# Scaling and transposing a normed input in one TensorE product with a diagonal matrix

## What is computed

```python
def rms_norm(x, gain, eps=1e-6):
    y = x * lax.rsqrt(jnp.mean(x * x, axis=-1, keepdims=True) + eps)
    return y * gain
# layer 0 (even) and layer 1 (odd), x: (1, 256, 1024)
h = rms_norm(x, mix_norm[l])          # one factor per row (frame), one gain per column
y = h @ w_in[l]                       # (1024, 2816) in layer 0, (1024, 3600) in layer 1
# the mixers, h @ w_out, the residual add and the MoE follow
```

## Time and profile before

| what | value |
|---|---|
| three runs | 620.03, 622.05, 623.84 us; median 622.05 |
| the profiled execution | 622.66 us, of which the span of the profile is 620.9 |
| mean granted TensorE clock | 0.958 of full |
| instructions | 11990 |
| DMA | 145.24 MB, mean 234 GB/s |

### The profile page before, as it was taken

One profiled execution on the slowest core, in us unless ns is written; L12 is line 12 of the kernel. 1 busy time (PEld: TensorE's weight loads), 2 busy tenths in 40 slices (PEclk: granted clock), 3 DMA queues, 4 the chain that ended last, 5 costly groups with the idle time before them and its releaser, 6 DMA issues.

```text
span 620.9 us, 11990 instructions
## 1 busy us (share of the span) xinstructions
PE 545.1 (88%) x5109; PEld 451.7 (73%) x5109; DVE 336.7 (54%) x593; ACT 245.2 (39%) x457; POOL 81.2 (13%) x99
## 2 busy tenths in 40 slices
PE   2899986779979888884999999999999989788986
PEld 2899985679756466641999999899989856366642
DVE  2456759974562333447599655546646562433355
ACT  3453555254433133314545642443324533133221
POOL 6600242410100000001200290001110100000000
PEclk9999997969898999999899979999998898999999
DMA  8995400013989999999565252000021999999992
GB/s 310 276 344 167 170 2 1 1 68 125 398 341 413 410 406 409 409 410 374 170 204 186 66 194 69 2 3 4 2 69 66 407 335 392 409 409 409 409 409 112
DMA packets 55893, 145.24 MB, mean 234 GB/s; under 512 B 4260, under 2 KB 29040, under 8 KB 55712
## 3 DMA queue, kind: packets, MB, share of 16 engines
q1 hardware_dynamic: 54752, 142.47, 60.7%
q0 software_dynamic: 1088, 2.00, 1.5%
HBM read 143.40 MB, written 1.05 MB: 233 GB/s over the span
## 4 chain that ended last, share of the span: by engine, by line
PE 76%; DVE 13%; ACT 5%; issue 4%; DMA 2%; POOL 1%; SPq 0%; DVEq 0%; ACTq 0%
PE PS L1830 11%; PE PS L510 7%; PE PS L1791 7%; PE PS L511 7%; PE PS L512 6%; PE PS L1852 6%; PE PS L1866 3%; PE PS L546 3%; PE PS L547 3%; PE PS L548 3%; DVE WL L506 2%; PE PS L1867 2%; DVE X L1100 2%; PE PS L2126 2%; DMA RAW<-ev_w_in 2%
## 5 line engine op out<-in xcount | busy, mean ns | idle before, releaser
L506 DVE TENSOR_TENSOR WL<-RAW,WH 128x768 fp32r<-128x768 f32 (+2 forms) x96 | 82.8, 906 | 59.0 <-ACT WH L500 57.8
L510 PE MATMUL PS<-WH,HTH 128*128 128x384 f32 (+2 forms) x272 | 91.8, 338 | 3.1 <-DVE HTL L1100 1.4
L511 PE MATMUL PS<-WL,HTH 128*128 128x384 f32 (+2 forms) x272 | 90.3, 332 | 0.0
L512 PE MATMUL PS<-WH,HTL 128*128 128x384 f32 (+2 forms) x272 | 90.1, 331 | 0.0
L1100 DVE TENSOR_TENSOR X<-PS,X 128x512 f32<-128x512 f32 (+2 forms) x84 | 52.4, 662 | 62.6 <-PE PS L1867 49.0
L500 ACT ACTIVATE WH<-RAW 128x768 fp32r<-128x768 f32 (+2 forms) x96 | 70.7, 796 | 18.2 <-PE PS L512 10.4
L510 PEld LDWEIGHTS PS<-WH,HTH 128*128 128x128 f32 x272 | 53.1, 195 | 4.7 <-DVE HTL L1100 2.2
L511 PEld LDWEIGHTS PS<-WL,HTH 128*128 128x128 f32 x272 | 53.1, 195 | 0.0
L512 PEld LDWEIGHTS PS<-WH,HTL 128*128 128x128 f32 x272 | 52.8, 194 | 0.0
L546 PE MATMUL PS<-HTH,WH 128*128 128x256 f32 x160 | 46.6, 291 | 3.8 <-DVE HTL L1100 3.8
L547 PE MATMUL PS<-HTL,WH 128*128 128x256 f32 x160 | 46.1, 288 | 0.0
(11 more groups left out here) (344 smaller groups left out, 1051.1 us busy)
## 6 DMA issues: line engine op xcount, KB each, us to landing
RAW<-moe_w_gate SPq DMA_DIRECT2D x32, 512.0 KB, 11.3
RAW<-moe_w_up SPq DMA_DIRECT2D x32, 512.0 KB, 12.3
RAW<-moe_w_down SPq DMA_DIRECT2D x32, 512.0 KB, 13.9
XG<-moe_w_gate SPq DMA_DIRECT2D x32, 512.0 KB, 14.3
XG<-moe_w_up SPq DMA_DIRECT2D x32, 512.0 KB, 14.7
XD<-moe_w_down SPq DMA_DIRECT2D x32, 512.0 KB, 14.7
RAW<-od_w_in SPq DMA_DIRECT2D x9, 1536.0 KB, 8.2
RAW<-ev_w_in SPq DMA_DIRECT2D x6, 1536.0 KB, 12.9
```

Source lines behind the costliest of these rows:

```text
L506: done(nc.vector.tensor_tensor(out=lo, in0=raw, in1=hi.bitcast(F32), op=ALU.subtract), "unit_lo")
L510: nc.tensor.matmul(ps, ah, bh, start=start, stop=False)
L511: nc.tensor.matmul(ps, ah, bl, start=False, stop=False)
L512: return nc.tensor.matmul(ps, al, bh, start=False, stop=stop)
```

## The change

X comes in two transfers, one for each tile. The identity and the gains (now GR, 16 rows of 128 for both layers, 8 KB) are fetched by ScalarE's queue. The first two of the eight k blocks of chunk 0 have a transfer of their own. TensorE transposes GR once, and ScalarE copies the result to GC, one column of gains per block k.

H is no longer computed. VectorE writes DGR, the identity times the row factors (128x128 for each tile), and TensorE computes X^T * diag(factor) as a plain float32 product of X (stationary) with DGR (moving), one PSUM bank of 128x256 per block k. ScalarE rounds it with the gain as its scale (`norm_hi`), VectorE takes the remainder in one instruction with the same gain (`norm_lo`). Both alternate with the weight units, and TensorE puts the products of unit j+2's input behind the matmuls of unit j. Before the first products TensorE runs 14 (layer 0) or 10 (layer 1) products of the identity with itself, whose result is not used (`warm`). In layer 1 the squares are taken in halves, each when its half of X is added, and VectorE norms before it takes the first weight unit instead of behind three. The broadcast of layer 1's gains is gone, and on GpSimd the two steps of `norm(0)` now come ahead of the masks' DMA.

The diff, with its indentation reduced by eight; left out are `MSQ`, `GC` and `GR`'s declarations, merged or renumbered semaphores (`mask`, `lb_d`, `pt`, `hT_ps`, `hT_hi` of the later projections), and the wait for `c_pad`, which moves from ahead of layer 1's projection into its evacuation:

```diff
@@ -155,7 +155,8 @@
...
 gb = top[0]
-GB = sb("GB", [P, D])
+top[0] += D * 4
+DGR = at("DGR", [P, NT, P], gb)
@@ -314,6 +316,7 @@
...
 PROJ_BANKS = 6
+NORM_BANK = (0, 1, 2, 3, 6, 7, 1, 2)
@@ -389,9 +392,8 @@
...
     xv = x.rearrange("b (i p) d -> p (b i) d", p=P)
-    sp.dma_start(X[:, :, :], xv).then_inc(sem("x_in"), 16)
-    sp.dma_start(CT[:, 0:P], consts[:, 0:P]).then_inc(sem("ct_in"), 16)
-    sp.dma_start(GB[:, :], mix_norm[0].partition_broadcast(P)).then_inc(sem("g0_in"), 16)
+    for i in range(NT):
+        sp.dma_start(X[:, i, :], xv[:, i, :]).then_inc(sem(f"x_in{i}"), 16)
@@ -423,8 +425,12 @@
...
                 sp.wait_ge(sem("unit_lo"), slot_units[i - SLOTS])
-            sp.dma_start(RAW[:, s, 0:KT * n].rearrange("p (k n) -> p k n", k=KT),
-                         w[0, :, c0:c0 + n].rearrange("(k p) n -> p k n", p=P)).then_inc(sem(f"landed{s}"), 16)
+            raw = RAW[:, s, 0:KT * n].rearrange("p (k n) -> p k n", k=KT)
+            src = w[0, :, c0:c0 + n].rearrange("(k p) n -> p k n", p=P)
+            if i == 0:
+                sp.dma_start(raw[:, 0:2], src[:, 0:2]).then_inc(sem("first"), 16)
+                raw, src = raw[:, 2:], src[:, 2:]
+            sp.dma_start(raw, src).then_inc(sem(f"landed{s}"), 16)
@@ -490,7 +496,9 @@
...
     u = unit_no[i, j]
-    if u == min(unit_no[i, jj] for jj in range(4)):
+    if u == 0:
+        act.wait_ge(sem("first"), 16)
+    elif u == 1 or i and u == min(unit_no[i, jj] for jj in range(4)):
@@ -602,29 +611,28 @@
...
     link(nc.gpsimd.memset(NH, -0.5))
+    link(nc.gpsimd.memset(MSQ.rearrange("p (i b) -> p i b", b=2)[:, :, 1:2], 0.0))
...
-    def gain(n, src):
-        pool.wait_ge(sem("dn"), downs(0, QUADS))
-        pool.dma_start(GB[:, :], src.partition_broadcast(P)).then_inc(sem("gb_in"), 16)
...
         for i in range(NT):
-            pool.wait_ge(sem("ms"), n + i + 1)
-            rsqrt(pool, link, "rs", RS[:, i:i + 1], MS[:, i:i + 1], MSE[:, i:i + 1], 1.0)
+            pool.wait_ge(sem("ms"), 2 + 2 * (i + 1) if n else i + 1)
+            link(nc.gpsimd.tensor_scalar(out=MSE[:, i:i + 1], in0=MSQ[:, 2 * i:2 * i + 1], scalar1=MSQ[:, 2 * i + 1:2 * i + 2],
+                                         scalar2=EPS, op0=ALU.add, op1=ALU.add))
+            done(nc.gpsimd.tensor_tensor(out=RS[:, i:i + 1], in0=MSE[:, i:i + 1], in1=NH[:, 0:1], op=ALU.pow), "rs")
...
+    norm(0)
     pool.dma_start(MKF[:, :, :], masks).then_inc(sem("mk_in"), 16)
-    norm(0)
@@ -698,16 +706,16 @@
...
         return
-    gain(2, mix_norm[1])
...
     residual_ready(pool, 2)
-    pool.wait_ge(sem("h"), 4)
+    pool.wait_ge(sem("hT_ps"), 13)
...
         rows = slice(CH * c, CH * c + CH)
+        pool.wait_ge(sem("hT_ps"), 20)
@@ -755,16 +763,28 @@
...
             if n == 0:
-                act.wait_ge(sem("x_in"), 16)
-            else:
-                residual_ready(act, n, i)
-            done(nc.scalar.activation(H[:, i, :], X[:, i, :], ACT.Square, scale=1.0 / 32,
-                                      accum_out=MS[:, i:i + 1]), "ms")
+                act.wait_ge(sem(f"x_in{i}"), 16)
+                done(nc.scalar.activation(H[:, i, :], X[:, i, :], ACT.Square, scale=1.0 / 32,
+                                          accum_out=MSQ[:, 2 * i:2 * i + 1]), "ms")
+                continue
+            for b in range(2):
+                act.wait_ge(sem("comb_x"), 4 * PARTS - 3 + 2 * i + b)
+                cs = slice(512 * b, 512 * b + 512)
+                done(nc.scalar.activation(H[:, i, cs], X[:, i, cs], ACT.Square, scale=1.0 / 32,
+                                          accum_out=MSQ[:, 2 * i + b:2 * i + b + 1]), "ms")
...
+    def norm_hi(layer, kb):
...
+        for k in (2 * kb, 2 * kb + 1):
+            act.wait_ge(sem("hT_ps"), 12 * layer + k + 1)
+            done(nc.scalar.activation(HTH[:, k, :], PS[:, NORM_BANK[k], 0:T], ACT.Copy,
+                                      scale=GC[:, KT * layer + k:KT * layer + k + 1]), "hT_hi")
@@ -789,22 +810,24 @@
...
-    def first_splits(layer):
-        for j in range(3):
-            split_hi(act, slot_of[layer, "in", 0], j)
+    def first_split(layer):
+        split_hi(act, slot_of[layer, "in", 0], 0)
...
             i = slot_of[layer, "in", c]
-            for j in range(3 if c else 0):
-                split_hi(act, i, j)
-                inside(c, j)
             if c == 0:
-                lhs_hi(2 * layer)
+                for j in range(4):
+                    norm_hi(layer, j)
+                    if j < 3:
+                        split_hi(act, i, j + 1)
             else:
+                for j in range(3):
+                    split_hi(act, i, j)
+                    inside(c, j)
                 evacuate(layer, c - 1)
-            split_hi(act, i, 3)
+                split_hi(act, i, 3)
@@ -906,22 +929,26 @@
...
+    act.dma_start(CT[:, 0:P], consts[:, 0:P]).then_inc(sem("gain_in"), 16)
+    act.dma_start(GR[0:2 * KT, :], mix_norm.rearrange("l (k p) -> (l k) p", p=P)).then_inc(sem("gain_in"), 16)
     norm(0)
-    first_splits(0)
+    act.wait_ge(sem("pt_ps"), 1)
+    act.wait_ge(sem("pt"), done(nc.scalar.activation(GC, PS[:, 7, 0:2 * KT], ACT.Copy), "pt"))
+    first_split(0)
@@ -1113,28 +1139,35 @@
...
     def norm(n):
-        dve.wait_ge(*((sem("gb_in"), 16) if n else (sem("g0_in"), 16)))
+        if n == 0:
+            dve.wait_ge(sem("gain_in"), 32)
...
             dve.wait_ge(sem("rs"), n + i + 1)
-            done(stt(H[:, i, :], X[:, i, :], RS[:, i:i + 1], GB[:, :], MUL, MUL), "h")
+            done(ts(DGR[:, i, :], ident, RS[:, i:i + 1], MUL), "dg")
...
+    def norm_lo(layer, kb):
+        for k in (2 * kb, 2 * kb + 1):
+            dve.wait_ge(sem("hT_hi"), 12 * layer + k + 1)
+            ins = stt(HTL[:, k, :], PS[:, NORM_BANK[k], 0:T], GC[:, KT * layer + k:KT * layer + k + 1],
+                      HTH[:, k, :].bitcast(F32), MUL, SUB)
+        done(ins, "hT_lo")
...
-    def first_splits(layer):
-        for j in range(3):
-            split_lo(dve, slot_of[layer, "in", 0], j)
+    def first_split(layer):
+        split_lo(dve, slot_of[layer, "in", 0], 0)
...
         for c in range(len(CHUNKS[layer])):
-            for j in range(3 if c else 0):
-                split_lo(dve, slot_of[layer, "in", c], j)
-            if c == 0:
-                lhs_lo(2 * layer)
-            split_lo(dve, slot_of[layer, "in", c], 3)
+            for j in range(4):
+                if c == 0:
+                    norm_lo(layer, j)
+                if c or j < 3:
+                    split_lo(dve, slot_of[layer, "in", c], j if c else j + 1)
@@ -1481,8 +1514,8 @@
...
         return
-    first_splits(1)
     norm(2)
+    first_split(1)
@@ -1719,13 +1752,38 @@
...
         if c == 1:
-            pe.wait_ge(sem("ct_in"), 32)
+            pe.wait_ge(sem("ct_in"), 16)
...
+    def norm_T(layer, kb):
...
+        for kk in range(2):
+            k = 2 * kb + kk
+            for i in range(NT):
+                if k == 0:
+                    pe.wait_ge(sem("dg"), 2 * layer + i + 1)
+                last = mm(PS[:, NORM_BANK[k], i * P:(i + 1) * P], X[:, i, k * P:(k + 1) * P], DGR[:, i, :],
+                          start=True, stop=True)
+            done(last, "hT_ps")
...
+    def warm(n):
+        for _ in range(n):
+            mm(PS[:, 6, 0:128], ident, ident, start=True, stop=True)
...
     def in_projection(layer, between):
-        lhs(lambda i, k: H[:, i, k * P:(k + 1) * P], lambda i: pe.wait_ge(sem("h"), 2 * layer + i + 1))
-        for c in range(len(CHUNKS[layer])):
+        if layer:
+            warm(10)
+        norm_T(layer, 0)
+        norm_T(layer, 1)
+        for j in range(4):
+            pe.wait_ge(sem("hT_lo"), 8 * layer + j + 1)
+            project_unit(pe, layer, "in", 0, j)
+            if j < 2:
+                norm_T(layer, j + 2)
+        between(0)
+        for c in range(1, len(CHUNKS[layer])):
@@ -1906,7 +1964,10 @@
...
-    pe.wait_ge(sem("ct_in"), 16)
+    pe.wait_ge(sem("gain_in"), 32)
+    done(nc.tensor.transpose(PS[:, 7, 0:2 * KT], GR[0:2 * KT, :], ident[0:2 * KT, 0:2 * KT]), "pt_ps")
+    warm(14)
```

More of the change, by code:

```diff
@@ L192, in program @@
         TA = m.take("TA", [P, NT, 768])
+        GR = at("GR", [P, P], m.at)
         TB = m.take("TB", [P, NT, 1024])
@@ L576, in bc @@
             return ap.unsqueeze(axis).to_broadcast(shape)
+        MSQ, GC = sm(4), sm(2 * KT)
         NH, MS, MSE, RS, MSC = sm(64), sm(2), sm(2), sm(2), sm(6)
@@ L651, in _ @@
                 rows = slice(CH * c, CH * c + CH)
-                link(nc.gpsimd.tensor_copy(MKC[rows, :, :], MKF[rows, 0:6, rows]), also="maskc")
+                link(nc.gpsimd.tensor_copy(MKC[rows, :, :], MKF[rows, 0:6, rows]), also="mask")
             link(nc.gpsimd.memset(RST[:, :], 1.0))
@@ L1620, in _ @@
             dve.wait_ge(sem("c_yi"), 2)
-            dve.wait_ge(sem("maskc"), 2)
+            dve.wait_ge(sem("mask"), 3)
             negated(0)
```

16 lines of the change are left out of this document (8 added, 8 removed).

## The result

The changed kernel runs in 616.77 us (median of 7 runs, 613.32 to 618.06), the kernel before in 623.37 (7 runs beside them): a ratio of 0.9898, 95% interval 0.9875 to 0.9921. A second set of 6 runs gave 615.66 and 0.9885 (0.9853 to 0.9917). The forecast of the median was 614.7, a gain of 7.4 us; by the two ratios it is 6.4 (4.9 to 7.8) and 7.2 (5.2 to 9.2). The size fits, but the profiles show that it came about otherwise: the two places that the forecast is made of gave 7.2, and an end that no step of it looked at took 1.6 back. All ratios here leave out runs more than 1.5% above the fastest of their kernel: one of the four of no_warm_l1 (the profiled one) and one of the ten of before_pad.

A forecast was written before the change was run, and what follows sets the result against it. TensorE was taken as the bound, 88% busy, with DMA full in the expert fetches. Gains of 4.9 (layer 0) and 2.5 us (layer 1) sum to 7.4, taking the median from 622.05 to 614.7 us, range 611.5 to 619.5.

The forecast's parts named there:

- Layer 0, predicted 4.9: Layer 0's first projection: chunk 0 ends at 23.5 us instead of 28.37, a gain of 4.9 us.
- bounds of 3.5 and 5.8: Layer 0's identity and gains: landing taken as 5.0 us; 3.5 would add 1.5 to the gain, 5.8 take 0.8.
- the 24 slow matmuls: Layer 0, first 24 projection matmuls, 0.211 us apart at the lower clock; speeding them up gives 2.2 us.
- hidden by this, with 2.8 us to spare: Layer 0's row factors, ready at 8.0 us, are covered by warm products lasting until 10.85.
- Layer 1, predicted 2.5: Layer 1's first projection: chunk 0 ends at 305.05 us, its read before began at 307.63; gain 2.5 us.
- Rival (a): Layer 1's warm products start at the lower clock; gain there only 0.6 to 0.7, total 616.6 us; chance 0.15.
- Rest of chunk 0: Layer 0's remaining chunk 0 weights land at 11.5 us; they must land by 13.3 for unit 1.
- (b): Layer 0's clock rises only behind unit 0, chunk end near 27, total 618 us; chance 0.1.
- (c): Layer 0's identity and gains land at 3.5 us, total 613.2 us; chance 0.14.
- (e): Slower: identity and gains starved, landing at 15 us, chunk 0 10 us later than forecast, total 624.7; chance 0.04.
- (d): A later stage, a fetch tied to the wall clock, takes the gain back, total 622 us; chance 0.05.
- what is gained in front of 17.39 us should arrive at the end undiminished: From layer 0's first projection onward: fetches follow compute, so the whole early gain reaches the end; likewise in layer 1.

The follow-up runs named there:

- no_warm_l1: The changed kernel without the 10 warm products ahead of layer 1's norm products; 615.99 us (4 runs), ratio 0.9863 to the kernel before.
- before_pad: The kernel before with 40 float32 64x64 products of a constant (160 TensorE instructions) added at TensorE's start; 623.93 us, ratio 1.002.
- clock_only: The kernel before with only warm identity products added, 12 planned in layer 0 and 19 in layer 1; 618.93 us, ratio 0.9943.
- no_warm_l0: The changed kernel without the 14 warm products of layer 0; 614.43 us, ratio 0.9847 to the kernel before.
- one_piece: The changed kernel with chunk 0 of layer 0's weights in one transfer of 1.5 MB; 615.92 us, ratio 0.9897 to the kernel before.
- one_queue: The changed kernel with identity and gains issued from SyncE's queue, behind X; 617.98 us, ratio 0.9898 to the kernel before.
- early64: The changed kernel with 38 float32 64x64 products ahead of the identity wait replacing layer 0's 14 warm ones; 611.65 us, ratio 0.9828 to the kernel before.

## Why the prediction was right, and where it was off

- **Layer 0, predicted 4.9, came out at 4.56** (4.3 between the means of two profiles each). Identity and gains landed at 5.5, the forecast took 5.0 from bounds of 3.5 and 5.8; this term is the one that was off. Warm products 5.34 us, from 5.71 to 11.05 (forecast 5.6, from 5.25 to 10.85), unit 0 at 13.19 (13.0), pace 0.12 throughout, first read 23.90 (23.6). The row factors' diagonal came at 8.83 and not at 8.0, since X landed 0.6 us later and GpSimd's steps have gaps; the warm products hid it.
- **What the 4.56 consist of was read wrongly.** The prediction put 2.2 of it down to the 24 slow matmuls that the warm products speed up. clock_only bears out that figure for the kernel before. In the changed kernel, however, the warm products stand between a diagonal that is ready at 8.8 and products that could use it, and no_warm_l0 has the first read at 23.41: the rest of the change alone gives 4.8 (28.21, the mean of the two profiles of before, less 23.41), and the warm products take 0.4 back. The row factors "hidden by this, with 2.8 us to spare" should have been read as a delay of over 2 us for products that were ready to run.
- **Layer 1, predicted 2.5, came out at 2.68.** Products 2.34 us behind the warm ones' start (forecast 2.4), no low clock, GpSimd's second pow 0.58 instead of 1.16. By the runs 1.4 to 1.5 of it is the shorter path and 1.24 the clock. Rival (a) did not come: TensorE was without work for only 0.48 us before the warm products. Left without them for 1.9 us, as in no_warm_l1, the clock did fall.
- **Hidden parts.** Rest of chunk 0: forecast 11.5, landed 10.5, and one_piece shows the split needn't be there. ScalarE's queue is worth 1.36 us by one_queue, more than the 0.8 that the prediction put on its later bound.
- **The rivals.** (b) fell (0.12 from the first matmul), (c) fell (landing at 5.5 and not 3.5), (e) fell (nothing starved), (d) fell by the repeated profiles.
- **The step that failed is in the sum**: "what is gained in front of 17.39 us should arrive at the end undiminished". It does, up to the last additions: 7.46 us in that pair, with 0.2 of chance in it. But the end itself got 1.6 us longer, by a cost that is in no row of before: TensorE's stream became 162 instructions longer, and a packet of instructions now meets the last output transfer. 4.56 + 2.68 - 1.56 = 5.7 is what these two profiles show of the change itself, inside both intervals of the measured gain, as 7.4 is. That the forecast comes so near is thus in part luck.
- **What stays open.** The ratios say more than the stretches do. Taking the first, fourth and last columns against the means of the two profiles of before, the changed kernel gives 5.5 and 5.1 us where its ratios say 6.4 and 7.2; clock_only 1.1 for 3.6 (2.1 to 5.0), no_warm_l0 5.9 for 9.5 (7.2 to 11.8), no_warm_l1 4.3 for 8.5 (4.8 to 12.3), early64 9.6 for 10.7 (7.9 to 13.4). All eleven comparisons lean the same way, by 0.7 to 4.2 us. One profile for each variant can't say whether the other three stretches became shorter or the two profiles of before are short of its usual run.

## What to carry to other kernels

Products that only keep TensorE's clock up belong where the engine has to wait anyway (before its inputs land, or in a gap between two stages); put in front of work that is ready they cost what they give. When a small change moves the end of a kernel by a microsecond or two without touching it, look at the last output transfer and for an instruction packet beside it, and vary the length of the longest stream, by half a packet and by a whole one, before believing any other cause. And profile both kernels twice before explaining a difference of 1 to 3 us in a stage that was not edited.

## What the runs showed of the hardware

- Packets of some 16 KB of instructions share the DMA engines with the data: in eight profiles of thirteen a 256 KB transfer took 3.6 to 3.9 us instead of 2.1, and its last 2 KB packets started as such a packet ended, within 0.02 us. Whether it happens was decided by the count of TensorE's instructions: not at 0 and 258 more than before, at 106 to 162 more in every profile; some 250 of TensorE's records went with one packet.
- The moments at which the granted clock falls and rises differ between executions of the same program: 0.77 against 0.92 over 22 us, in a stretch that took 3.3 us longer at 0.77.
- float32 products of 64x64 (76 records in 5.94 us, 0.078 each) raise the clock as those of 128x128 do: the norm products behind them ran 14 records in 1.83 us, without them in 3.36.
